# Second block: pool branch projected before the convolution branch, the convolution's mean and variance inside that projection, all four pools ahead of the last channel tile

## The reference, cut to what matters

```python
proj = h @ w_in + b_in                       # 3584 columns
p = proj[..., :512]                          # pool branch
a = proj[..., 512:1536]                      # convolution branch
g = proj[..., 1536:]                         # 2 x 1024 gates
# pool branch: four groups of 128 channels, windows 2, 4, 8, 16
mixed = causal_window_mean(p, w) - p         # per group
y_pool = ((mixed @ pool_w[group]) * pool_scale) @ pool_up
# convolution branch
glu = a[..., :512] * sigmoid(a[..., 512:])
y = causal_depthwise_conv(glu, 31 taps) + dw_bias
y = layernorm(y, ln_g, ln_b); y = y * sigmoid(y)
y_conv = y @ conv_out
merged = sigmoid(g[..., :1024]) * y_pool + sigmoid(g[..., 1024:]) * y_conv
x = x + gate1 * (merged @ w_out)
```

## Time and profile before

| what | value |
|---|---|
| median of three runs | 3167.92 us |
| the profiled execution | 3173.78 us |
| its span, first to last instruction | 3171.7 us |
| mean granted clock of TensorE | 0.988 of full |
| TensorE busy | 3067.8 us |
| VectorE busy | 1595.6 us |
| ScalarE busy | 1150.7 us |
| GpSimd busy | 1755.0 us |

### The profile page before, as it was taken

How to read it: one execution, slowest core, us unless ns; L and a number is a source line. 1 busy time by engine, 2 the same in 40 slices (tenths; PEclk the granted TensorE clock), 3 DMA queues, 4 the chain that set the end, 5 groups by cost and what they waited for, 6 DMA issues and landing times.

```text
span 3171.7 us, 44168 instructions
## 1 busy us (share of the span) xinstructions
PE 3067.8 (97%) x14616; PEld 2495.4 (79%) x14616; DVE 1595.6 (50%) x2794; ACT 1150.7 (36%) x1478; POOL 1755.0 (55%) x2024
## 2 busy tenths in 40 slices
PE   7988999999999999988999999999999999999998
PEld 4777788877678888766788888888888888888887
DVE  6863555322545541994309997444411444454443
ACT  4354322236532222423333234555543332233232
POOL 1723677645057765773446665444445666666663
PEclk8999999999999999999999999999999999999999
DMA  8511455422045553221224445555564655556652
GB/s 338 184 46 54 158 190 189 155 77 92 21 135 190 190 182 101 88 93 54 87 87 134 145 132 180 189 195 182 177 241 141 225 195 192 180 181 204 205 193 78
DMA packets 170201, 481.94 MB, mean 152 GB/s; under 512 B 15360, under 2 KB 48896, under 8 KB 168080
## 3 DMA queue, kind: packets, MB, share of 16 engines
q1 hardware_dynamic: 147680, 410.83, 39.3%
q10 hardware_dynamic: 22448, 70.14, 5.6%
HBM read 411.70 MB, written 69.21 MB: 152 GB/s over the span
## 4 chain that ended last, share of the span: by engine, by line
PE 56%; issue 20%; POOL 18%; DVE 3%; ACT 1%; DMA 0%; DVEq 0%; POOLq 0%; SPq 0%; ACTq 0%
PE ps L1672 52%; POOL w_lo L552 18%; PE pa L1672 4%; DVE s_acc L1451 1%; DMA e_g<-expert_act 0%; DVEq L1448 0%; DVE s_tmp L1517 0%; DVE mg_lo L1519 0%; ACT mg_hi L923 0%; DVE s_m L1515 0%; DVE x L1127 0%; DVE s_gl L1439 0%; ACT L620 0%; POOLq L550 0%; POOLq L556 0%
## 5 line engine op out<-in xcount | busy, mean ns | idle before, releaser
L552 POOL TENSOR_TENSOR w_lo<-raw,w_hi 128x256 fp32r<-128x256 f32 x2020 | 1754.8, 900 | 1387.3 <-ACT w_hi L570 1385.8
L1672 PE MATMUL ps<-h_hi,w_hi 128*128 128x512 f32 x2392 | 946.4, 396 | 24.1 <-POOL w_lo L552 11.3
L1672 PE MATMUL ps<-h_hi,w_lo 128*128 128x512 f32 x2392 | 936.7, 392 | 0.0
L1672 PE MATMUL ps<-h_lo,w_hi 128*128 128x512 f32 x2392 | 912.4, 390 | 0.0
L570 ACT ACTIVATE w_hi<-raw 128x1024 fp32r<-128x1024 f32 x509 | 538.8, 1060 | 808.2 <-PE ps L1672 687.1
L1672 PEld LDWEIGHTS ps<-h_hi,w_hi 128*128 128x128 f32 x2392 | 451.9, 189 | 126.0 <-issue 18.3
L1672 PEld LDWEIGHTS ps<-h_hi,w_lo 128*128 128x128 f32 x2392 | 451.7, 189 | 95.8
L1672 PEld LDWEIGHTS ps<-h_lo,w_hi 128*128 128x128 f32 x2392 | 451.6, 189 | 92.9 <-issue 1.0
L1672 PE MATMUL ps<-wa_hi,w_hi 128*128 128x512 f32 x1024 | 398.5, 389 | 1.3 <-DVE x L1636 1.3
L1672 PE MATMUL ps<-wa_hi,w_lo 128*128 128x512 f32 x1024 | 398.4, 389 | 0.0
L1672 PE MATMUL ps<-wa_lo,w_hi 128*128 128x512 f32 x1024 | 398.4, 389 | 0.0
(11 more groups left out here) (322 smaller groups left out, 3072.7 us busy)
## 6 DMA issues: line engine op xcount, KB each, us to landing
ada<-in_ada SPq DMA_DIRECT2D x144, 512.0 KB, 4.4
raw<-in_expert_u SPq DMA_DIRECT2D x128, 512.0 KB, 4.1
raw<-in_expert_v SPq DMA_DIRECT2D x128, 512.0 KB, 4.1
raw<-in_ffn_in SPq DMA_DIRECT2D x88, 512.0 KB, 3.5
expert_act<-g_act ACTq DMA_DIRECT2D x128, 256.0 KB, 4.2
gate_matrix<-w_st ACTq DMA_DIRECT2D x16, 2048.0 KB, 6.7
e_w<-gate_matrix SPq DMA_DIRECT2D x16, 2048.0 KB, 11.3
e_g<-expert_act SPq DMA_DIRECT2D x128, 256.0 KB, 7.7
```

Source lines behind the costliest of these rows:

```text
L552: last = nc.gpsimd.tensor_tensor(w_lo[:, k, c:c + 256], raw[:, k, c:c + 256], w_hi[:, k, c:c + 256].bitcast(F32), ALU.subtract)
L1672: return nc.tensor.matmul(out, a, b, start=start, stop=stop_)
```

## The change

The two 512-deep projections change places: `pool_up` is loaded and multiplied first, then `conv_out`. The four mixes follow tiles 22 and 24 of `sec_in`, the mean follows the fourth half tile of `pool_up` and the variance the sixth. VectorE does all four pools before `begin(3)`, and the `pm_lo` parts before the last 15 taps; the gate products of `pool_up` are spread over the waits of the layer norm, and the merge is done with the `conv_out` tiles. ScalarE does `s_pm` and `pm_hi` between the gate tiles, and squares, `rstd` and SiLU after the last gate tile.

```diff
--- before.py
+++ after.py
@@
     ("ffn0_in", 44), ("ffn0_out", 24),
     ("mla_in", 6), ("mla_q", 6), ("mla_k", 2), ("mla_v", 2), ("mla_out", 8),
     ("ffn1_in", 44), ("ffn1_out", 24),
-    ("sec_in", 28), ("conv_out", 4), ("pool_up", 4), ("sec_out", 8),
+    ("sec_in", 28), ("pool_up", 4), ("conv_out", 4), ("sec_out", 8),
     ("query", 16), ("expert_u", 128), ("expert_v", 128),
 )
 
@@
     ("ffn0_in", 44), ("ffn0_out", 8),
     ("mla_in", 6), ("mla_qn", 8), ("mla_qr", 4), ("mla_k", 8), ("mla_v", 8), ("mla_out", 8),
     ("ffn1_in", 44), ("ffn1_out", 8),
-    ("sec_a", 8), ("sec_p", 4), ("sec_g", 16), ("conv_out", 8), ("pool_up", 8), ("sec_out", 8),
+    ("sec_a", 8), ("sec_p", 4), ("sec_g", 16), ("pool_up", 8), ("conv_out", 8), ("sec_out", 8),
     ("query", 16), ("expert_u", 128), ("expert_v", 128),
 )
 
@@
         sp_segment(sp, "mla_v", A["mla_v"], 1024)
         sp_segment(sp, "mla_out", A["mla_out"], 1024)
         sp_ffn(sp, 1)
-        for name in ("sec_in", "conv_out", "pool_up", "sec_out"):
+        for name in ("sec_in", "pool_up", "conv_out", "sec_out"):
             sp_segment(sp, name, A[name], 1024)
         sp_segment(sp, "query", A["query"], 1024)
         mu = M0["expert_u"]
@@
 
 
 
-    MEAN_AT, VAR_AT = 24, 25
+    MIX_AT = {22: (0, 1), 24: (2, 3)}
+    MEAN_AT, VAR_AT = 3, 5
 
     def act_second(act, hi):
         m, T = M0["sec_in"], T0["sec_a"]
@@
                 nc.scalar.activation(s_p[:, t - 8, PPAD:], bank, ACT.Identity, bias=col("b_in", t - 8)).then_inc(tile_free, 1)
             else:
                 nc.scalar.activation(s_sg[:, t - 12, :], bank, ACT.Sigmoid, bias=col("b_in", t)).then_inc(tile_free, 1)
-            if t == MEAN_AT + 1:
-                for k in range(4):
-                    act.wait_ge(cx, k + 1)
-                    nc.scalar.activation(s_csq[:, k, :], s_acc[:, k, :], ACT.Square).then_inc(csq, 1)
-            if t == VAR_AT + 1:
-                nc.scalar.preload_act_table_set(LN_EXP)
-                act.wait_ge(cvar, 1)
-                act.wait_ge(fin_ready, DT)
-                own_a.link(act, nc.scalar.activation(rstd[:, :], pa[:, 1, :], ACT.Ln, scale=1.0 / CW, bias=EPS))
-                nc.scalar.activation(rstd[:, :], rstd[:, :], ACT.Exp, scale=-0.5).then_inc(crs, 1)
+            for g in MIX_AT.get(t - 1, ()):
+                act.wait_ge(pw_mm, g + 1)
+                if g >= 2:
+                    act.wait_ge(mix_done, 4)
+                own_a.link(act, nc.scalar.activation(s_pm[g], pa[:, 2 + g % 2, :], ACT.Copy, scale=col("pool_scale", g)))
+                nc.scalar.activation(pm_hi[:, g, :], s_pm[g], ACT.Copy).then_inc(pmh, 1)
+        hi.upto(M0["pool_up"] + 3)
+        for k in range(4):
+            act.wait_ge(cx, k + 1)
+            nc.scalar.activation(s_csq[:, k, :], s_acc[:, k, :], ACT.Square).then_inc(csq, 1)
+        nc.scalar.preload_act_table_set(LN_EXP)
+        act.wait_ge(cvar, 1)
+        act.wait_ge(fin_ready, DT)
+        own_a.link(act, nc.scalar.activation(rstd[:, :], pa[:, 1, :], ACT.Ln, scale=1.0 / CW, bias=EPS))
+        nc.scalar.activation(rstd[:, :], rstd[:, :], ACT.Exp, scale=-0.5).then_inc(crs, 1)
+        hi.upto(M0["conv_out"])
         for t in range(4):
             act.wait_ge(ct, t + 1)
             own_a.link(act, nc.scalar.activation(s_acc[:, t, :], s_acc[:, t, :], ACT.Silu, bias=col("ln_b", t)))
             nc.scalar.activation(cy_hi[:, t, :], s_acc[:, t, :], ACT.Copy).then_inc(cyh, 1)
-        for g in range(4):
-            hi.upto(M0["conv_out"] + g // 2 + 3)
-            act.wait_ge(pw_mm, g + 1)
-            if g >= 2:
-                act.wait_ge(mix_done, 4)
-            own_a.link(act, nc.scalar.activation(s_pm[g], pa[:, 2 + g % 2, :], ACT.Copy, scale=col("pool_scale", g)))
-            nc.scalar.activation(pm_hi[:, g, :], s_pm[g], ACT.Copy).then_inc(pmh, 1)
-        hi.upto(M0["pool_up"] + 3)
+        hi.upto(M0["conv_out"] + 3)
         for k in range(DT):
-            hi.upto(M0["pool_up"] + k // 2 + 4)
+            hi.upto(M0["conv_out"] + k // 2 + 4)
             act.wait_ge(mgt, k + 1)
             nc.scalar.activation(mg_hi[:, k, :], s_tmp[:, k % 2, :], ACT.Copy).then_inc(mgh, 1)
 
@@
                                            in1=s_acc[:, t, :], op0=ALU.mult, op1=ALU.add).then_inc(conv_done, 1)
             done[0] += n * HALF
 
-        begin(0)
-        taps((0, 1))
-        for t in range(1, 4):
-            begin(t)
-            taps((t - 1, 1 + HALF), (t, 1))
-        taps((3, 1 + HALF))
-
         def pool(g, w):
 
             dve.wait_ge(tile_free, T0["sec_p"] + g + 1)
@@
                                    op0=ALU.mult, op1=ALU.subtract)
             v.tensor_tensor(s_mix[:, g, 0:PPAD], mean0, s_p[:, g, PPAD:2 * PPAD], ALU.subtract).then_inc(mix_done, 1)
 
-        pool(0, WINDOWS[0])
-        pool(1, WINDOWS[1])
+        begin(0)
+        taps((0, 1))
+        for t in range(1, 4):
+            if t == 3:
+                for g in range(4):
+                    pool(g, WINDOWS[g])
+            begin(t)
+            taps((t - 1, 1 + HALF), (t, 1))
+        for g in range(4):
+            dve.wait_ge(pmh, g + 1)
+            v.tensor_tensor(pm_lo[:, g, :], s_pm[g], pm_hi[:, g, :].bitcast(F32), ALU.subtract).then_inc(pml, 1)
+        taps((3, 1 + HALF))
         assert done[0] == 4 * CK
+
+        def pool_up(a, b):
+            for k in range(a, b):
+                dve.wait_ge(blk_done, M0["pool_up"] + k // 2 + 1)
+                v.tensor_tensor(s_sg[:, k, :], s_sg[:, k, :], ps[:, (T0["pool_up"] + k) % RING, :], ALU.mult)\
+                  .then_inc(tile_free, 1)
+
+        dve.wait_ge(tile_free, T0["pool_up"])
+        pool_up(0, 2)
         dve.wait_ge(conv_done, 4 * CK)
         dve.wait_ge(cmu, 1)
         for t in range(4):
             v.scalar_tensor_tensor(out=s_acc[:, t, :], in0=pa[:, 0, :], scalar=-1.0 / CW, in1=s_acc[:, t, :],
                                    op0=ALU.mult, op1=ALU.add).then_inc(cx, 1)
-        pool(2, WINDOWS[2])
+        pool_up(2, 6)
         dve.wait_ge(crs, 1)
         dve.wait_ge(cx, 4)
         for t in range(4):
@@
         for t in range(4):
             dve.wait_ge(cyh, t + 1)
             v.tensor_tensor(cy_lo[:, t, :], s_acc[:, t, :], cy_hi[:, t, :].bitcast(F32), ALU.subtract).then_inc(cyl, 1)
-        pool(3, WINDOWS[3])
-
-        def conv_out(a, b):
-            for k in range(a, b):
-                dve.wait_ge(blk_done, M0["conv_out"] + k // 2 + 1)
-                v.tensor_tensor(s_sg[:, DT + k, :], s_sg[:, DT + k, :], ps[:, (T0["conv_out"] + k) % RING, :], ALU.mult)\
-                  .then_inc(tile_free, 1)
-
-        dve.wait_ge(tile_free, T0["conv_out"])
-        conv_out(0, 4)
-        for g in range(4):
-            dve.wait_ge(pmh, g + 1)
-            v.tensor_tensor(pm_lo[:, g, :], s_pm[g], pm_hi[:, g, :].bitcast(F32), ALU.subtract).then_inc(pml, 1)
-        conv_out(4, DT)
-
-        T = T0["pool_up"]
+        pool_up(6, DT)
+
+        T = T0["conv_out"]
         dve.wait_ge(tile_free, T)
         for k in range(DT):
-            dve.wait_ge(blk_done, M0["pool_up"] + k // 2 + 1)
-            v.tensor_tensor(s_m2[:, :], s_sg[:, k, :], ps[:, (T + k) % RING, :], ALU.mult).then_inc(tile_free, 1)
+            dve.wait_ge(blk_done, M0["conv_out"] + k // 2 + 1)
+            v.tensor_tensor(s_m2[:, :], s_sg[:, DT + k, :], ps[:, (T + k) % RING, :], ALU.mult).then_inc(tile_free, 1)
             dve.wait_ge(tile_free, T + k + 1)
-            v.tensor_tensor(s_tmp[:, k % 2, :], s_m2[:, :], s_sg[:, DT + k, :], ALU.add).then_inc(mgt, 1)
+            v.tensor_tensor(s_tmp[:, k % 2, :], s_m2[:, :], s_sg[:, k, :], ALU.add).then_inc(mgt, 1)
             dve.wait_ge(mgh, k + 1)
             v.tensor_tensor(mg_lo[:, k, :], s_tmp[:, k % 2, :], mg_hi[:, k, :].bitcast(F32), ALU.subtract).then_inc(mg_done, 1)
         dve_residual(dve, "sec_out", 1, 5, 6)
@@
             for k in range(DT):
                 last = unit(out, (m + t) % RING, k * P, h_hi[:, k, :], h_lo[:, k, :], k == 0, k == DT - 1)
             last.then_inc(blk_done, 1)
-            if t == MEAN_AT:
-                pe.wait_ge(conv_done, 4 * CK)
-                for k in range(4):
-                    last = mm(pa[:, 0, :], ones, s_acc[:, k, :], k == 0, k == 3)
-                last.then_inc(cmu, 1)
-            if t == VAR_AT:
-                pe.wait_ge(csq, 4)
-                for k in range(4):
-                    last = mm(pa[:, 1, :], ones, s_csq[:, k, :], k == 0, k == 3)
-                last.then_inc(cvar, 1)
+            for g in MIX_AT.get(t, ()):
+                mix(g)
+
+        def mean():
+            pe.wait_ge(conv_done, 4 * CK)
+            for k in range(4):
+                last = mm(pa[:, 0, :], ones, s_acc[:, k, :], k == 0, k == 3)
+            last.then_inc(cmu, 1)
+
+        def variance():
+            pe.wait_ge(csq, 4)
+            for k in range(4):
+                last = mm(pa[:, 1, :], ones, s_csq[:, k, :], k == 0, k == 3)
+            last.then_inc(cvar, 1)
```

(8 more changed lines are left out.)

## The result

The changed kernel took 3148.95 us (median of four runs, 3146.63 to 3151.54), the kernel before 3167.91 (four runs). The ratio is 0.9936, 95% interval 0.9924 to 0.9949: 16 to 24 us faster, 19.0 by the medians. The prediction said 3147.3, with 3143 to 3158 as range.

The account below looks back on a forecast made before the run. TensorE, busy 97% of the span, was taken as the bound: 21.4 us of waits go, 5.5 come, 3.9 of slow clock goes, 19.8; by merge start 20.6, so 3167.9 - 20.6 = 3147.3 us, range 3143 to 3158.

Parts of the forecast that it names:

- four pools beside GpSimd: VectorE ahead of begin(3): 11.4 us undisturbed times 1.42 for GpSimd's share makes 16.2 us, bounds 11.4 and 21.
- tile 3's input and the 30 steps: VectorE from begin(3) to the first step of tile 3 alone: duration kept as before, that point moving from 1409.83 to 1426.0.
- wait for `pm_hi` and four `pm_lo`: VectorE ahead of the last 15 steps: no wait, half a microsecond to spare; four pm_lo 4.1 us, range 2.8 to 4.6.
- last 15 steps: VectorE at the convolution's end: 15.5 us as before, bounds 14.0 and 17.5, GpSimd having about one and a half blocks beside.
- wait for squares: TensorE before the variance: the 2.9 us wait goes, the squares being hidden with 2.3 us to spare.
- wait for `cy_lo`: TensorE before conv_out: 4.1 us, where it was 6.4, with the slow clock expected behind it.
- the fast price: TensorE at mean and variance: eight f32 records at the 2.4 GHz level cost 3.44 us.
- late end: Pools 21, pm_lo 4.6, last steps 17.5, an 8.7 us wait, mean and variance slow again: gain 9.5, 3158.4 us.
- Rival 1: VectorE pays much more beside GpSimd; TensorE waits 4 to 9 us for the mean, clock slow: 3153 to 3158, chance 0.16.
- Rival 2: Gain lost again: the wait for cyl grows or a conv_out block comes late; slack 2.4 us; 3162 to 3170, chance 0.07.
- Rival 3: Each VectorE pass with two SBUF inputs waits out a whole GpSimd quarter, 0.69 us alone: 3167 us, chance 0.05.
- Rival 4: Waits at 1444 and 1463 leave TensorE at 1.2 GHz to the end of conv_out: slower, 3184 us, chance 0.04.

Follow-up runs that it names:

- e1: The kernel before with only the four pools moved ahead of begin(3) on VectorE, everything else as before: 3184.7 us, ratio 1.0045.
- e2: The kernel before with only ScalarE's order changed: squares after gate tile 24, rstd, SiLU and rounding after gate tile 25; conv_out still first: 3156.2 us, ratio 0.9957.
- e8: The changed kernel with ScalarE converting the next weight block before its pool passes (s_pm, pm_hi) behind gate tiles 23 and 25: 3148.7 us, ratio 0.9929.

## Why the prediction was right, step by step

Sums are taken from the start of `sec_in`, 1275.2 in the forecast and 1272.3 in the profile.

| step | forecast | measured |
|---|---|---|
| four pools beside GpSimd | 16.2 | 18.7 |
| tile 3's input and the 30 steps | 32.8, as before | 25.2 |
| wait for `pm_hi` and four `pm_lo` | 0 + 4.1 | 2.0 + 3.6 |
| last 15 steps | 15.5 | 17.3 |
| end of the convolution | 170.4 | 168.7 |
| TensorE at the mean | 169.0 | 168.7 |
| its wait there | 1.4 | none seen on TensorE, 0.3 on its weight load |
| wait for squares | none | none |
| wait for `cy_lo` | 4.1 | 4.1 |
| `conv_out` starts | 192.4 | 190.9 |
| from there to the first merge | 7.7 | 8.3 |
| stretch | 200.1 | 199.2 |

**The mechanism** held at each point where the profile could contradict it. The 12.1 and 2.9 us waits went, 4.1 of 6.4 stayed, the clock was 1.00 at the mean and 0.50 at `conv_out`, and the tail brought the gain through. That it is the cover and not the placement of the pools is shown by e1 (the pools alone cost 15.2 us). But the prediction gave the whole saving to what TensorE does meanwhile, and e2 shows that this holds for the first wait alone: the waits for squares and for `cy_lo` stood behind ScalarE's gate tiles, and with the branches in their old order they go as well, for 13.3 us. The prediction did not weigh that.

**The terms** were less good than their sum. The prediction said that pools could cost up to 21 and took 16.2; the row it chose, the last pool of the kernel before, ends with GpSimd idle again (1469.3) and a piece of 0.17. It took the last steps at 15.5 with "one and a half blocks" beside them; GpSimd worked throughout. The excess sits in the 16-column pieces above all, 0.6 to 0.7 us where GpSimd is at work against 0.17. It said there would be no wait for `pm_hi`, "with half a microsecond to spare"; it was 2.0 us. These are 6 us too little in all (2.5 + 1.5 + 1.8). It took the 30 steps as they were, and with tile 3's input they were 7.6 us faster. The step that failed is the silent one: the pace of steps that were moved was carried over from where they had stood, and nothing was said about it. The last two of these excesses and the windfall are no independent errors: the lock-out that let VectorE run gave GpSimd a backlog, which then lay beside the last 15 steps (1.15 us each, all of them), and the early end of the 30 steps is what made VectorE wait for `pm_hi`. e8, without the lock-out, has 28.2 us for the 30 steps, no wait for `pm_hi`, and the convolution 1.3 us later. That the end of the convolution was hit within 2 us is therefore in part luck; that the time was hit is less so, since e8 took 3148.7 us.

One reading of the rows was wrong. The 5.97 and 4.82 us that the prediction gives to the eight products of the mean and of the variance are TensorE's busy time in windows that cut both groups short. The groups themselves took 6.5 and 5.4 us:

```profile
1425.43 6.51 PE L1672 MATMUL pa<-s_acc,consts 128*128 128x512 f32 x8 [12.11 <-DVE s_acc L1451]
...
1440.28 5.40 PE L1672 MATMUL pa<-s_csq,consts 128*128 128x512 f32 x8 [2.85 <-ACT s_csq L901]
```

In the changed kernel they took 3.7 and 3.6, so the slow clock had cost 4.6 us there and not 3.9. The forecast itself goes by the fast price (3.44 each) and is not touched; its late end would be about a microsecond later.

**The rivals.** Rival 1 (the wait for the mean grows) did not come, but there was no slack: the last step ended at 1440.97, the mean started at 1441.03, and its weight load waited 0.3 us. Rival 2 did not come; the slack it named is there. Rival 3 (full blocking at every pass) is wrong as a pace, a median quarter is 1.18 us, and yet the lock itself showed, in the other direction: GpSimd was the one kept out, for 9.0 us. The Trainium skill (SBUF — State Buffer, Who interferes with whom) says that the order of issue decides which engine blocks. The runs agree as far as they go: with the same instructions on VectorE, GpSimd was locked out or not as its block came at one time or another (the changed kernel, e8). Rival 4 (a lasting low clock) did not come; the low level at `conv_out` lasted about 5 us.

**The total.** 3147.3 forecast, 3149.0 measured, and 3146.8 in the repeat: the difference of the two is as large as the error.

## What to carry to other kernels

A wait at a reduction can be filled by work of another branch, even when the way there makes the reduction later: here the convolution ended 18.5 us later and the kernel gained 19. But before such a turn, look at the in-order waits ahead of the dependent steps on the engines that only help; a few moved lines on ScalarE gave 13.3 us by themselves. And where VectorE and GpSimd both read SBUF, a duration taken from one place in the profile holds only for that place, since the pace of either depends on when the other comes back from its pause.
